# Two slab steps woven with three steps of the delta rule, in place of four with five, in the first mixer of a hybrid block pair

## The reference

```python
def hybrid_mixer(h, w_in, conv_qkv_w, a_log, dt_bias, gdn_norm_w, conv_short_w, w_out):
    p = h @ w_in
    qkv = jax.nn.silu(causal_depthwise_conv(p[..., Q_OFF:Z_OFF], conv_qkv_w))
    ...
    o = gated_delta_rule_chunked(l2_normalize(q), l2_normalize(k), v, g, beta)
    o = rms_norm(o, gdn_norm_w) * jax.nn.silu(z.astype(jnp.float32))
    y_gdn = o.reshape(bsz, s, GDN_WIDTH).astype(h.dtype)
    y_sc = sc_b * causal_depthwise_conv(sc_c * sc_h, conv_short_w)
    return jnp.concatenate([y_gdn, y_sc], axis=-1) @ w_out
```

## Time and profile before

| | us |
|---|---|
| median of 3 runs | 2085.97 (2085.11 to 2091.56) |
| profiled execution, its own time | 2089.39 |
| its span | 2088.2 |
| TensorE busy | 1940.8 (93%) |
| GpSimd, ScalarE, VectorE busy | 954.8, 710.3, 686.0 |

### The profile page before, as it was taken

The page is one execution under the profiler, slowest core; times in us unless marked ns, Lnnn a source line. Parts: engine busy times, 40 slices in busy tenths (PEclk is TensorE's granted clock), DMA queues, the critical chain, the costliest instruction groups (busy, mean ns, idle before and its releaser), DMA issues.

```text
span 2088.2 us, 32887 instructions
## 1 busy us (share of the span) xinstructions
PE 1940.8 (93%) x13928; PEld 1655.1 (79%) x13928; DVE 686.0 (33%) x1069; ACT 710.3 (34%) x1093; POOL 954.8 (46%) x1257
## 2 busy tenths in 40 slices
PE   5989998999999999999999899977777799999997
PEld 4667776777888889999999899966666478888885
DVE  5654454223111102332210156544554422222101
ACT  2563222332222323222222334354445432322222
POOL 3543232545545665554545465421112265555563
PEclk9999999999999999999999999988989899999998
DMA  7332231233333232223222322000000323323221
GB/s 281 123 135 87 67 104 65 81 111 121 121 91 96 91 96 91 91 92 91 89 88 88 126 91 87 31 7 2 2 2 2 131 81 103 99 91 96 90 100 58
DMA packets 54690, 182.75 MB, mean 88 GB/s; under 512 B 6512, under 2 KB 6768, under 8 KB 54416
## 3 DMA queue, kind: packets, MB, share of 16 engines
q1 hardware_dynamic: 54544, 180.65, 26.6%
HBM read 175.39 MB, written 5.24 MB: 87 GB/s over the span
## 4 chain that ended last, share of the span: by engine, by line
PE 83%; DVE 6%; ACT 4%; DMA 3%; issue 2%; POOL 1%; SPq 1%; DVEq 0%; ACTq 0%
PE PS L498 69%; PE PS L615 3%; PE PS L969 1%; DMA RAWS<-w_w_in 1%; DMA ADA<-w_ada 1%; PE PS L962 1%; POOL WL L2171 1%; PE PS L976 1%; DMA BON<-bsave 1%; PE PS L987 1%; PE PS L533 1%; DMA RAWS<-w_f0g 1%; PE PS L634 0%; DVE HL L1585 0%; PE PS L943 0%
## 5 line engine op out<-in xcount | busy, mean ns | idle before, releaser
L2171 POOL TENSOR_TENSOR WL<-RAWS,WH 128x256 fp32r<-128x256 f32 x1074 | 824.2, 798 | 780.2 <-ACT WH L1666 780.1
L498 PE MATMUL PS<-HH,WH 128*128 128x264 f32 (+2 forms) x2184 | 668.8, 348 | 42.6 <-POOL WL L2171 9.4
L498 PE MATMUL PS<-HL,WH 128*128 128x264 f32 (+2 forms) x2184 | 655.3, 342 | 0.0
L498 PE MATMUL PS<-HH,WL 128*128 128x264 f32 (+2 forms) x2184 | 653.1, 341 | 0.0
L498 PEld LDWEIGHTS PS<-HH,WH 128*128 128x128 f32 (+1 forms) x2184 | 377.7, 190 | 108.6 <-issue 22.7
L1666 ACT ACTIVATE WH<-RAWS 128x1024 fp32r<-128x1024 f32 (+2 forms) x275 | 283.7, 1033 | 475.2 <-PE PS L498 401.1
L498 PEld LDWEIGHTS PS<-HH,WL 128*128 128x128 f32 (+1 forms) x2184 | 378.4, 190 | 48.4 <-issue 0.6
L498 PEld LDWEIGHTS PS<-HL,WH 128*128 128x128 f32 (+1 forms) x2184 | 378.9, 190 | 47.7 <-issue 2.1
L498 PE MATMUL PS<-IHf,WH 128*128 128x512 f32 (+1 forms) x704 | 209.4, 338 | 0.0
L498 PE MATMUL PS<-IHf,WL 128*128 128x512 f32 (+1 forms) x704 | 209.3, 338 | 0.0
L498 PE MATMUL PS<-ILf,WH 128*128 128x512 f32 (+1 forms) x704 | 209.2, 338 | 0.0
(11 more groups left out here) (498 smaller groups left out, 1814.7 us busy)
## 6 DMA issues: line engine op xcount, KB each, us to landing
RAWS<-w_w_in SPq DMA_DIRECT2D x52, 512.0 KB, 4.4
RAWS<-w_ada SPq DMA_DIRECT2D x32, 512.0 KB, 3.6
RAWS<-w_f0g SPq DMA_DIRECT2D x22, 512.0 KB, 3.6
RAWS<-w_f0u SPq DMA_DIRECT2D x22, 512.0 KB, 3.7
RAWS<-w_f1g SPq DMA_DIRECT2D x22, 512.0 KB, 3.6
RAWS<-w_f1u SPq DMA_DIRECT2D x22, 512.0 KB, 3.5
RAWS<-w_f2g SPq DMA_DIRECT2D x22, 512.0 KB, 3.5
RAWS<-w_f2u SPq DMA_DIRECT2D x22, 512.0 KB, 3.6
```

The lines of the kernel that those rows point to most:

```text
L498: ins = te.matmul(ps[0:m, q, o:o + b - a] if len(halves) > 1 else ps[0:m, o:o + b - a], w[:, k * m:k * m + m], v[:, k0 + k, a:b], start=fi ...
L2171: ins = ge.tensor_tensor(WL[s % NS][:, p], RAW[i % NR][:, p], WH[s % NS][:, p].bitcast(f32), ALU.subtract)
```

## The change

One number and one pattern, the latter on all four engines that compute:

```diff
-DELTA_TICKS = 25
+DELTA_TICKS = 30
...
         pr, dr = project_rest(), later_by(DELTA_TICKS, pipeline(4, prepare, scan))
-        alternate(pr, pr, dr, dr, pr, pr, dr, dr, dr)
+        alternate(pr, dr, dr, pr, dr)
```

## The result

| | before | with the change |
|---|---|---|
| median of 7 runs each | 2085.97 us (2083.06 to 2091.56) | 2099.33 us (2096.88 to 2107.99) |
| ratio | | 1.0062, 95% interval 1.0044 to 1.0081 |
| span of the profiled execution | 2088.2 | 2106.8 |
| from the first L680 to the first `w_out` matmul | 207.8 | 230.6 |

The change made the kernel slower by 0.6%, 2 us more than forecast and inside the range. Behind the stretch the two traces agree: from the first `w_out` matmul to the end 1729.4 us before, 1730.2 after.

What follows compares the result with a forecast made beforehand. TensorE, busy for 93% of the span, was taken to bound the kernel. Terms 6.6 + 4.7 + 1.4 - 1.2 gave +11.5 us, so 2097.5 us against the median of 2085.97; range 2087 to 2106.

Steps and rivals of the forecast that it cites:

- Breaks: TensorE in the woven stretch: 26 more interruptions of the slabs at 0.19 us, 11 lost L615 joins at 0.15: +6.6 us.
- The last scan: VectorE's queue at the last block: a slab weighing ahead of WT and a convolution ahead of VN lengthen TensorE's waits: +4.7 us.
- the ST term: Last scan: L738 before the second L744 has only one step over the update of ST: +0.35 us.
- Elsewhere: VectorE's queue in the rest of the stretch: waits for LD, VBT, STG, VN and an exponential change: +1.4 us together.
- Behind the stretch: First `w_out` matmul's wait for HL falls from 2.8 to 1.6 us, as the delta rule ends earlier: -1.2 us.
- The clock: Lower-level time gained behind the HL wait is paid again in the last scan: 0 together, bounds -1.5 to +3 us.
- The clock rival: Single slab steps between small groups lower TensorE's clock some 8 more times, also in the inverse: +10 us, 2108 us; chance 0.08.
- my 1.5 us: Eight matmuls behind the 2.8 us HL wait take 3.4 us at the lower clock, 1.9 at the full level.
- the forecast of 13 us for the stretch: From first L680 to the start of the `w_out` matmuls: some 13 us more than the 207.8 of before.
- Half of that: Rival: breaks and VectorE's queue cost half of the forecast: +2.6 us, 2088.6 us, no change; chance 0.20.
- The finer weave covers the waits: Rival: slab steps behind small groups hide waits for VN, VBT, STG, RSTD, WT: -6.6 us, 2079.4 us; chance 0.04.

Runs made afterwards that it cites:

- e3: The changed kernel with VectorE's last ada-slab weighing and slab 23's convolution put off to the middle of slab 24: 2096.56 us, 1.0050.
- e1: The changed kernel's two-to-three rate in a coarser pattern (pr, pr, dr, dr, dr) on all engines: 2104.17 us, 1.0081 of the kernel before.
- e5: The changed kernel with TensorE alone on the coarser pattern (pr, pr, dr, dr, dr), other engines keeping the changed order: 2112.96 us, 1.0111.
- e6: The kernel before with TensorE alone on a finer pattern of single steps, other engines keeping the old order: 2095.99 us, 1.0046.
- e12: The changed kernel itself run and profiled again, for its clock: 2098.97 us, 1.0057 of the kernel before.
- e11: The kernel before with VectorE's gated output of the last block put behind the last convolution by ten empty steps: 2085.89 us, 1.0002.
- e9: The kernel before with VectorE computing each VN five times over, so TensorE waits idle longer in all eight chunks: 2118.14 us, 1.0144.
- e4: The kernel before with DELTA_TICKS 30 in place of 25, the delta rule beginning four slab steps later: 2101.19 us, 1.0061.
- e8: The kernel before with DELTA_TICKS 20 in place of 25, the delta rule beginning four slab steps earlier: 2098.14 us, 1.0051.
- e10: The kernel before with each VN computed five times and ten unread slab matmuls filling each of TensorE's eight VN waits: 2107.49 us, 1.0097.

## Why the prediction was right, point by point

*The total* was right: 2097.5 forecast, 2099.33 measured. In the traces it is made of other terms than forecast.

1. **Breaks, +6.6: confirmed in size.** The stretch of the changed kernel holds 78 runs of slab matmuls, 52 before; at the full clock a run costs 0.20 us over 0.233 per matmul (70 runs, 14.2 us; before, 49 runs, 9.9 us): 26 x 0.20 = +5.2. L615 takes 29.6 us before and 30.7 in e3, where all its groups run at full clock: 11 more groups, +1.1, 0.10 each in place of 0.15. Together 6.3. A three between groups takes 0.89 us, as forecast:

```profile
191.88 0.50 PE L498 MATMUL PS<-HH,WH 128*128 128x512 f32 x1
...
192.77 0.68 PE L615 MATMUL PS<-iv0UD,iv0XU 64*64 64x64 f32 x16
```

The coarser kernels e1 and e5 don't contradict the price; they show that it can't be saved by itself. e6 is the nearest to a test of it by time, 1.0046 for 23 more breaks and no more waiting.

2. **The last scan, +4.7: the mechanism was right, the size half.** WT 2.2 (forecast 2.3); VN 3.0 (3.7), since the convolution took 332.97 - 329.48 = 3.49 us here and not 4.05, L1209 in it 0.59 and not 0.95; the ST term 0 (0.35), nothing shows; last L756 1.1 (2.1). That wait does hold copy and square, as forecast, but the two take 1.0 us together, not 2.1:

```profile
347.94 0.38 ACT L1886 ACTIVATE QKV<-PS 128x256 f32<-128x256 f32 x1 [7.96 <-PE PS L751]
348.35 0.63 ACT L1892 ACTIVATE RSTD<-QKV 128x512 f32<-128x512 f32 x1
...
349.03 1.22 PE L756 MATMUL PS<-RSTD,KC 128*128 128x512 f32 x1 [1.14 <-ACT RSTD L1892]
```

From 4.1 for the three to 6.3: +2.2.

3. **Elsewhere, +1.4: measured +3.5.** LD +1.6 as forecast (0.7 and 0.95). VBT +0.4 instead of -0.2, STG -1.1 (-0.9), VN of the fourth chunk nothing (+0.7). What was missed: MOD (+1.5). A slab of the first mixer waits until VectorE has read the ada sum out of its bank (L1061), and that read now stands behind a state update (L1334) and two operations of the next `prepare` (L1284, L1286). I had followed the queue for the delta rule's operations only. AT was +1.1, not 0.15 (0.8 in e12). With point 2 the two are 5.7 us against 6.1 forecast: a shortfall of 2.5 and an excess of 2.1 that cancel by luck.

4. **Behind the stretch, -1.2: exact.** HL 1.6 in place of 2.8; e11 did the same to the kernel before, with the same 1.6.

5. **The clock, 0 with bounds -1.5 to +3: wrong for the traces, within its bounds for the median as far as can be told.** In both profiled executions of the changed kernel the rest is 11 to 12 us, and of what was looked at only the clock accounts for it: 27.3 us more at half speed cost at most 13.7, an estimate for a TensorE that is never idle. The clock rival had the size (+10) but the wrong place: the inverse, where single slab steps stand between small groups, kept 1.00 (165 to 211 us), and the falls came elsewhere, over half of their time from the last scan on (13.7 and 6.8 of 34.1 us). What I had wrong: a wait of 3.6 us ahead of L744 makes that chunk of e9 cost 3.9 us over the wait (8.65 against 4.75). I had taken my 1.5 us from one wait, 2.8 us for HL, with nothing but slabs behind it; behind VN stand L744, L748 and L751, behind which the clock falls in both kernels even with no wait ahead.

Then why was the total right? The medians differ by 13.4 us (first runs) and 11.9 (e12's batch). Breaks (6.3) and waits (4.5) are 10.8 of them, and these were forecast at 11.5; that leaves 1 to 3 us for the clock and everything else. The thirteen clocks on record agree with so little: 3 us more at the lower level, where a microsecond of it costs 0.3 to 0.5. The traces have 22.8 us in the stretch because both profiled executions (2107.99, 2103.46) lay at the slow, low-clock end of their series; the forecast of 13 us for the stretch missed them for this reason. In which executions the clock falls at these places, and why not in all, stays open.

*The rivals.* "Half of that" is out, the interval begins at 1.0044. "The finer weave covers the waits" is out: of the five waits it names only STG (1.4 to 0.3) and RSTD (1.3 to 1.1) shrank, and breaks cost 0.20, not under 0.1. e1 and e5 show the opposite, that waits grow when TensorE's order is made coarser against VectorE's.

## What to carry to other kernels

Price an interruption of a matmul stream from its own rows (here 0.20 us each) and multiply it by the count from the order of instructions; that price is the same in the traces of e1, e5, e6 and both runs of the changed kernel. Walk the queue of the engine that answers for every waiter, also the ones outside the woven part (MOD was such), because a moved start alone (e4, e8: 0.5 to 0.6%) can cost as much as a changed pattern. A wait on the bound engine can cost its length and as much again by the clock behind it: 3.6 us of wait and 3.9 behind it in e9's trace, 31 us in its median for 13.5 us of waiting. The changed kernel, with one such wait, shows nearly nothing of it in the median. So look at the granted clock of several executions before a loss in one trace is taken for a loss in time.

## What the runs showed of the hardware that was not expected

- The falls of the clock come back at the same places: two profiles of the changed kernel have the 13.7 us one at the same instruction, and e11 repeats both falls of the kernel before. The clocks of the timed executions (0.961 to 0.974 for one kernel) show that they don't have the same amount of it.
- Giving TensorE 20 us of useless matmuls in its waits made the program 10.6 us faster than leaving it idle there (e10 against e9).
- 32 small matmuls (L533, 128x1) near the start take either 6.83 us or about 4, with the same instructions ahead of them in all kernels: 6.83 in 8 of the 14 profiles, among them the kernel before, 3.7 to 4.0 in the other 6, among them both of the changed kernel. It is the clock: in the short ones a matmul takes 0.25 us while the record shows the upper level (34.2 to 37.6 us in the changed kernel) and 0.35 around that; in the long ones each takes 0.35 and the record of the clock begins only at 52 to 54 us. Up to there the view prints 1.00, although the slab matmuls at 44 us last 0.63, as at the lower level elsewhere (0.40 at the upper). Why the clock rises early in some executions stays open; it makes 2.8 us of noise between them.

```profile
33.50 6.83 PE L533 MATMUL PS<-KC,ACC 128*128 128x1 f32 x32
...
44.40 0.63 PE L498 MATMUL PS<-HL,WH 128*64 128x512 f32 x1
```

In the changed kernel:

```profile
33.47 4.00 PE L533 MATMUL PS<-KC,ACC 128*128 128x1 f32 x32
```
